# A transformer layer on one core: where the recurrent heads' element-wise work runs, on GpSimd, VectorE and ScalarE, and what it waits for

## The reference

```python
h = rms_norm(x, attn_norm_g)
qd, kd, vd, qr, fr, ir, gr = split(h @ w_in)             # 7 parts of 512 columns
od = rms_norm(diff_attention(norm(qd), norm(kd), vd, lam), subln_g) * (1 - lam_init)
lf = log_sigmoid(fr); kr = -expm1(lf); qr = silu(qr)     # recurrence: 4 heads, chunks
orr = hgrn2_chunked(qr, kr, ir, lf)                      # S_t = diag(f_t) S_(t-1) + k_t v_t^T
orr = rms_norm(orr, hgrn_norm_g) * silu(gr)
x = x + concat(od, orr) @ w_out
h = rms_norm(x, ffn_norm_g)
x = x + (silu(h @ w_gate) * (h @ w_up)) @ w_down
```

## Time and profile before

| what | value |
|---|---|
| median of the runs | 2820.31 us |
| the profiled execution's own time | 2819.41 us |
| its span | 2817.7 us |
| PE busy in the span | 2643.6 us (94%) |
| DVE, ACT, POOL busy | 1496.2, 1104.5, 758.5 us (53, 39, 27%) |
| granted PE clock, mean | 0.974 of full speed |

### The profile page before, as it was taken

One profiled execution on the slowest core, in us unless ns is written; L12 is line 12 of the kernel. 1 busy time (PEld: TensorE's weight loads), 2 busy tenths in 40 slices (PEclk: granted clock), 3 DMA queues, 4 the chain that ended last, 5 costly groups with the idle time before them and its releaser, 6 DMA issues. The chain is left out here.

```text
span 2817.7 us, 34114 instructions
## 1 busy us (share of the span) xinstructions
PE 2643.6 (94%) x13384; PEld 2235.7 (79%) x13384; DVE 1496.2 (53%) x1887; ACT 1104.5 (39%) x1871; POOL 758.5 (27%) x527
## 2 busy tenths in 40 slices
PE   7999999995999999987995999998999997999999
PEld 6888888885888888875884888887888886888887
DVE  5434343431676767663336655667566664456643
ACT  4434343331566666663234222224222222423221
POOL 5000000001424141400003544445544442146400
PEclk9999999997999999998997999999999998999999
DMA  4545455455443433206655333335333343787763
GB/s 162 196 164 179 136 183 176 148 179 157 107 105 105 105 106 83 76 8 207 194 198 202 112 103 100 104 102 196 109 100 104 101 112 91 254 293 253 253 213 126
DMA packets 338673, 415.78 MB, mean 148 GB/s; under 512 B 18513, under 2 KB 212049, under 8 KB 336721
## 3 DMA queue, kind: packets, MB, share of 16 engines
q1 hardware_dynamic: 338512, 413.60, 47.0%
HBM read 291.38 MB, written 122.16 MB: 147 GB/s over the span
## 5 line engine op out<-in xcount | busy, mean ns | idle before, releaser
L1846 PE MATMUL gate_bank<-gate_b_hi,gate_a_hi 128*128 128x512 f32 x1232 | 482.6, 392 | 37.1 <-DVE first_b_lo L1726 21.8
L1848 PE MATMUL gate_bank<-gate_b_hi,gate_a_lo 128*128 128x512 f32 x1232 | 481.4, 391 | 0.0
L1847 PE MATMUL gate_bank<-gate_b_lo,gate_a_hi 128*128 128x512 f32 x1056 | 412.4, 391 | 0.0
L1846 PEld LDWEIGHTS gate_bank<-gate_b_hi,gate_a_hi 128*128 128x128 f32 x1232 | 232.8, 189 | 87.5 <-issue 22.8
L1848 PEld LDWEIGHTS gate_bank<-gate_b_hi,gate_a_lo 128*128 128x128 f32 x1232 | 232.6, 189 | 48.6
L525 PE MATMUL proj_prod<-proj_w_hi,proj_h_hi 128*128 128x512 f32 x640 | 253.1, 395 | 6.8 <-DVE proj_w_lo L380 6.1
L2124 PE MATMUL down_prod<-down_w_hi,down_f_hi 128*128 128x512 f32 x616 | 241.4, 392 | 18.4 <-DVE down_f_lo L2060 18.2
L380 DVE TENSOR_TENSOR proj_w_lo<-proj_w_raw,proj_w_hi 128x2048 fp32r<-128x2048 f32 x56 | 128.7, 2299 | 230.1 <-ACT proj_w_hi L280 230.1
L527 PE MATMUL proj_prod<-proj_w_hi,proj_h_lo 128*128 128x512 f32 x640 | 250.1, 391 | 0.0
L526 PE MATMUL proj_prod<-proj_w_lo,proj_h_hi 128*128 128x512 f32 x640 | 249.8, 390 | 0.0
L2125 PE MATMUL down_prod<-down_w_lo,down_f_hi 128*128 128x512 f32 x616 | 240.7, 391 | 0.0
(11 more groups left out here) (212 smaller groups left out, 5548.8 us busy)
## 6 DMA issues: line engine op xcount, KB each, us to landing
proj_w_raw<-in_w_in_dram SPq DMA_DIRECT2D x56, 1024.0 KB, 6.4
first_full<-in_w_gate_dram SPq DMA_DIRECT2D x88, 256.0 KB, 3.9
gate_full<-in_w_up_dram SPq DMA_DIRECT2D x88, 256.0 KB, 4.0
ff<-gate_ff_sum SPq DMA_DIRECT2D x88, 256.0 KB, 2.9
down_w_raw<-in_w_down_dram SPq DMA_DIRECT2D x22, 1024.0 KB, 7.5
down_f_raw<-ff SPq DMA_DIRECT2D x56, 384.0 KB, 3.3
down_f_raw<-ff SPq DMA_DIRECT2D x56, 320.0 KB, 3.5
gate_b_lo<-operands SPq DMA_DIRECT2D x12, 1024.0 KB, 9.5
```

The lines of the kernel that those rows point to most:

```text
L1846: pe.matmul(dst, a_hi[:, pos, s, :], b_hi[pos][:, s, :], start=opens and s == 0, stop=False, skip_group_check=True)
L1847: pe.matmul(dst, a_hi[:, pos, s, :], b_lo[pos][:, s, :], start=False, stop=False, skip_group_check=True)
L1848: last = pe.matmul(dst, a_lo[:, pos, s, :], b_hi[pos][:, s, :], start=False, stop=s == HALF_SLABS - 1, skip_group_check=True)
```

## The change

Three things change in `mix_tokens`:

1. The recurrent chunks (4 to 7) are scaled by DVE instead of ACT: one TENSOR_TENSOR of 128x512 for each chunk, with `rec_o` and the inverse roots as inputs, in place of four ACT instructions of 128x128. It stands at the end of DVE's step, one step ahead of the transposition. In the last head ACT scales all four attention chunks before it copies the first chunk; before, it scaled one chunk ahead.
2. On POOL, `behind_combination` is gone, and so is the gate's wait for the combination.
3. On POOL, all seven factors of a head are made at the head's start, behind the gate of the head before.

```diff
--- before.py
+++ after.py
@@ -822,53 +822,29 @@
 
         @block.gpsimd
         def _(pool):
-            def product(h, m):
-                src = whole[m][:] if m else rf[:].rearrange("p h n -> p (h n)")
-                src = src.rearrange("p (n s) -> p n s", s=2)
-                if m:
-                    pool.wait_ge(whole_made, h * LEVELS + m)
-                nc.gpsimd.tensor_tensor(whole[m + 1][:], src[:, :, 0], src[:, :, 1], ALU.mult).then_inc(whole_made, 1)
-
-            def behind_combination(h, n):
-
-                step = h * STEPS + n // 2
-                if n % 2 == 0 and step:
-                    pool.wait_ge(combined, step)
-
-            def gate(h):
-                pool.wait_ge(rgate_in, 16 * (h + 1))
-                pool.wait_ge(fill_read, filled(h, len(FILLS) - 1))
-                if h + 1 < HEADS:
-                    pool.wait_ge(combined, (h + 1) * STEPS - 1)
-                nc.gpsimd.tensor_tensor(ro[:], ro[:], rgate[:], ALU.mult).then_inc(r_gated, 1)
-
             for h in range(HEADS):
-                if h == 0:
-                    pool.wait_ge(rf_in, 16)
-                    for m in range(LEVELS):
-                        product(h, m)
+                pool.wait_ge(rf_in, 16 * (h + 1))
+                for m in range(LEVELS):
+                    src = whole[m][:] if m else rf[:].rearrange("p h n -> p (h n)")
+                    src = src.rearrange("p (n s) -> p n s", s=2)
+                    if m:
+                        pool.wait_ge(whole_made, h * LEVELS + m)
+                    nc.gpsimd.tensor_tensor(whole[m + 1][:], src[:, :, 0], src[:, :, 1], ALU.mult).then_inc(whole_made, 1)
                 for side in range(2):
                     pool.wait_ge(fill_done, filled(h, fill_at("diagonal", side, HALF - 1)))
                     nc.gpsimd.tensor_tensor(half(rq, side), half(rq, side), half(rf, side), ALU.mult).then_inc(q_ready[side], 1)
                 for m in range(LEVELS):
                     for side in range(2):
-                        n = fill_at("level", side, m)
-                        pool.wait_ge(fill_done, filled(h, n))
-                        behind_combination(h, n)
+                        pool.wait_ge(fill_done, filled(h, fill_at("level", side, m)))
                         if m:
                             pool.wait_ge(k_ready[side], h * LEVELS + m)
                         nc.gpsimd.tensor_tensor(runs_of(rk, side, m, 0), runs_of(rk, side, m, 0), factor(side, m, 0), ALU.mult).then_inc(k_ready[side], 1)
                         pool.wait_ge(q_ready[side], h * UPDATES + m + 1)
                         nc.gpsimd.tensor_tensor(runs_of(rq, side, m, 1), runs_of(rq, side, m, 1), factor(side, m, 1), ALU.mult).then_inc(q_ready[side], 1)
-                if h + 1 < HEADS:
-                    pool.wait_ge(k_ready[1], (h + 1) * LEVELS)
-                    pool.wait_ge(q_ready[1], (h + 1) * UPDATES)
-                    pool.wait_ge(rf_in, 16 * (h + 2))
-                    for m in range(LEVELS - 1):
-                        product(h + 1, m)
-                    pool.wait_ge(fill_read, filled(h, len(FILLS) - 1))
-                    product(h + 1, LEVELS - 1)
-                gate(h)
+                pool.wait_ge(rgate_in, 16 * (h + 1))
+
+                pool.wait_ge(fill_read, filled(h, len(FILLS) - 1))
+                nc.gpsimd.tensor_tensor(ro[:], ro[:], rgate[:], ALU.mult).then_inc(r_gated, 1)
 
         @block.scalar
         def _(act):
@@ -927,19 +903,9 @@
                 nc.scalar.activation(o_rms[:], o_sumsq[:], ACT.Sqrt, bias=eps[:], scale=1.0 / P).then_inc(o_rms_made, 1)
 
             def normalise(h, c):
-
-                if c < TURNS:
-                    act.wait_ge(o_rrms_made, h + 1)
-                    for t in range(c * GROUP, (c + 1) * GROUP):
-                        nc.scalar.activation(o_all[h % 2][:, t, :], o_all[h % 2][:, t, :], ACT.Copy, scale=o_rrms[:, t:t + 1]).then_inc(o_normed, 1)
-                else:
-                    act.wait_ge(r_rrms_made, h + 1)
-                    act.wait_ge(r_gated, h + 1)
-                    head = c - TURNS
-                    for t in range(CH):
-                        part = ro[:, t, head * C:(head + 1) * C]
-                        at = t * HEADS + head
-                        nc.scalar.activation(part, part, ACT.Copy, scale=ro_rrms[:, at:at + 1]).then_inc(r_scaled, 1)
+                act.wait_ge(o_rrms_made, h + 1)
+                for t in range(c * GROUP, (c + 1) * GROUP):
+                    nc.scalar.activation(o_all[h % 2][:, t, :], o_all[h % 2][:, t, :], ACT.Copy, scale=o_rrms[:, t:t + 1]).then_inc(o_normed, 1)
 
             act.wait_ge(chain, 2)
             nc.scalar.activation(lam_exps[:], lam_dots[:], ACT.Exp).then_inc(lam_exp_made, 1)
@@ -966,13 +932,13 @@
                 if 0 < len(groups) <= 2:
                     read_output(s - 1)
                 if s == TOTAL + 1:
-                    normalise(HEADS - 1, 0)
+                    for c in range(TURNS):
+                        normalise(HEADS - 1, c)
                 for head, c in chunks_at(s):
-                    if s == TOTAL + 1 and c + 1 < CHUNKS:
-                        normalise(head, c + 1)
                     take_chunk(head, c)
                 for head, c in chunks_at(s + 1) if s < TOTAL else ():
-                    normalise(head, c)
+                    if c < TURNS:
+                        normalise(head, c)
 
         @block.vector
         def _(dve):
@@ -1035,6 +1001,16 @@
                 nc.vector.reciprocal(ro_rrms[:], ro_rms[:]).then_inc(r_rrms_made, 1)
                 dve.wait_ge(o_rms_made, h + 1)
                 nc.vector.reciprocal(o_rrms[:], o_rms[:]).then_inc(o_rrms_made, 1)
+
+            def normalise(h, c):
+
+                if c >= TURNS:
+                    dve.wait_ge(r_rrms_made, h + 1)
+                    dve.wait_ge(r_gated, h + 1)
+                    head = c - TURNS
+                    out = ro[:, :, head * C:(head + 1) * C]
+                    scale = ro_rrms[:].rearrange("p (c h) -> p c h", h=HEADS)[:, :, head]
+                    nc.vector.tensor_tensor(out, out, scale.unsqueeze(2).to_broadcast([P, CH, C]), ALU.mult).then_inc(r_scaled, 1)
 
             nc.vector.memset(state[:], 0.0)
             nc.vector.memset(early[:].bitcast(F32), 0.0).then_inc(masks_made, 1)
@@ -1068,6 +1044,8 @@
                     read_fill(h, 2 * j + 1)
                 if live and h and j == FIRST_CHUNK_STEP - 2 or s == TOTAL + 1:
                     invert_roots(h - 1)
+                for head, c in chunks_at(s + 1) if s <= TOTAL - 1 else chunks_at(s):
+                    normalise(head, c)
 
         @block.tensor
         def _(pe):
@@ -1118,7 +1096,7 @@
                 if c < TURNS:
                     pe.wait_ge(o_normed, h * STEPS + (c + 1) * GROUP)
                 else:
-                    pe.wait_ge(r_scaled, (h * HEADS + c - TURNS + 1) * CH)
+                    pe.wait_ge(r_scaled, h * HEADS + c - TURNS + 1)
                 open_slot(slot)
                 for t in range(GROUP):
                     src = o_all[h % 2][:, c * GROUP + t, :] if c < TURNS else ro[:, t, (c - TURNS) * C:(c - TURNS + 1) * C]
```

## The result

The change makes the kernel slower: 2838.47 us, median of 4 runs (2837.49 to 2840.85), against 2820.68 us, median of 4 runs before (2819.41 to 2823.25). The ratio is 1.0063 (1.0046 to 1.0081), +17.8 us. The forecast was 2844 us in a range of 2826 to 2854.

What follows compares the result with a forecast made beforehand. PE, busy 94% of the span, was taken as the bound, so new PE waits are time. 13.8 + 2.1 + 2.8 + 6.9 - 3.3 + 2.4 = 24.7 us slower than 2819.4 gave 2844 us, range 2826 to 2854.

Steps and rivals of the forecast that it cites:

- Step 5 of part 1: Heads 1 to 3: late DVE scalings let POOL's products hold L1000 and L1004; PE stalls 2.4 us, booked as 2.3 each.
- part 2: POOL's level products no longer wait for the combination: 2.1 us at step 7 plus 2.8 us at step 8.
- Step 6 of part 1: Heads 1 to 3, one step on: the same hold with a slightly shorter one on the second scaling, 2.3 us each.
- clock term: PE falls to its 1.2 GHz level after new waits: two more drops, 2.4 us, bounds 0 to 10.8.
- the clock falls after each new wait: Rival: 7 more clock drops of PE than taken, +8.4 us, 2852.5 us; chance 0.11.
- Step 7: All four heads: POOL's product or L1004 first, a draw; 0 or 1.05 us each, half taken, 2.1 us.
- Step 8: All four heads: POOL goes first, L1004 ends 1.05 us later, PE stalls 0.7 each; 2.8 us.
- Head ends: Three head ends: the next head's factor products hold L1000 and L1004, 2.3 us late each; 6.9 us.
- End of the stage: Last head: ACT scales 16 times, then copies, DVE scaling beside it; -3.3 us, bounds -5.5 and -1.7.
- The scalings slip through: Rival: both DVE scalings run ahead of POOL's q product, part 1's cost is zero; +9.3 us, 2829 us; chance 0.18.
- DVE is hardly held: Rival: DVE's queued pair L1000, L1004 keeps its turn against POOL; +1.8 us, 2821 us; chance 0.11.
- Faster, through ACT: Rival: ACT's lighter load shrinks PE's 26.2 us of waits for exponentials; 2801.5 us, or 2816 with the end alone; chance 0.05.

Runs made afterwards that it cites:

- scaling_alone: Kernel before, with only the recurrent chunks' scaling moved to DVE and the changed end of the stage; POOL as before: 2819.86 us, ratio 0.9995.
- wait_restored: Changed kernel, but POOL's side 0 level products wait for the combination again: 2823.80 us, ratio 1.0013 to the kernel before.
- one_input: Changed kernel, but in the first three heads DVE's scalings become sums over the same 128x512 elements with one SBUF input: 2825.80 us, ratio 1.0020 to before.
- act_scaling_in_heads: Changed kernel, but ACT does the recurrent scaling within the heads again; the end stays as changed: 2828.15 us, ratio 1.0030 to the kernel before.
- no_wait_alone: Kernel before, with only the wait of POOL's level products for the combination removed: 2827.96 us, ratio 1.0025.
- factors_alone: Kernel before, with only all seven factors made behind the gate and the gate's wait for the combination removed: 2826.20 us, ratio 1.0018.
- end_alone: Kernel before, with only the last head's eight chunks scaled as in the changed kernel: 2819.17 us, ratio 0.9993.
- end_all_dve: Kernel before, with DVE scaling all eight chunks of the last head, one instruction each, ACT only copying: 2814.61 us, ratio 0.9981.

## Why the prediction was right

The sign, the size and the order of the engines came out. Step by step:

**Step 5 of part 1** was right in mechanism and size: 2.2 us measured, 2.4 worked out and 2.3 booked. The chain is the one that the prediction wrote down: turns at step 4, k ahead of the small instruction, q ahead of the combination. But it hangs on both parts. By `scaling_alone` and `wait_restored` the late pair itself costs 0.59 us; the other 1.63 us are the holds on L966 (0.84) and L970 (0.79), which need part 1 to make DVE late and part 2 to let POOL go. The trace of after has POOL ahead by 0.05 us (865.51 against 865.56). The prediction booked the whole under part 1, and in the sum that made no difference. It had a margin that wasn't there: with DVE 1.1 us late its k product came 0.55 us ahead of L1000 (862.1 against 862.65), while in the trace DVE is 0.59 late and POOL 0.05 to 0.07 ahead. At step 6 a lead of 0.13 us for DVE was enough to turn the order, so the prediction was lucky that POOL still came first at step 5.

**Step 6 of part 1** was right in size by luck and wrong in cause. 2.3 each were forecast from a second hold. In the trace L966 and L970 keep their bare lengths there (0.22 and 1.02 us): behind the second pair DVE still waits for PE's scores (2.17, 1.20 and 1.84 us in heads 1 to 3), so the pair doesn't make it late, and the 3.3, 1.6 and 3.3 us come from PE at 1.2 GHz for 6.8, 3.4 and 6.8 us. The prediction's clock term (two drops, 2.4 us) was too small for steps 5 and 6, and the rival "the clock falls after each new wait" was right for the 2.1 us waits: it fell after three of three. It was wrong for the waits of 1.3 us and less: at steps 7 and 8 and at the head ends the kernel after has no drop. So two errors of about the same size offset each other: the hold of 6.9 that did not come, and a clock loss of 8.2 that did. For both steps and the clock together 16.2 us were forecast (13.8 + 2.4) and 14.8 measured (6.6 + 8.2). That the wait brings the drop about rests on its coming in three heads of three in the one profiled execution of the kernel after, and in none of the heads of `scaling_alone`, `wait_restored`, `one_input` and `act_scaling_in_heads`, where that wait is missing.

**Step 7** was called a draw and priced at half. POOL won it four times of four in the kernel after and again in `no_wait_alone`: 3.4 us for 2.1.

**Step 8**: 0.80 each, 3.2 us for 2.8.

**Steps 9 and 10** were not in the sum. They give back 5.5 us. Some 0.2 in each head is part of the hold of step 8 given back: `no_wait_alone` has the same 0.22, and so has head 3, behind which there are no factors to make. Part 3 gives next to nothing: the factor products no longer run beside the combination of step 9, whose L1004 took 1.86 us and in `factors_alone` takes 1.42, but `wait_restored`, which has part 3 without the hold, gains 0.05 us in head 2, where neither it nor before had a drop. The prediction took 0 for it. The rest is a clock drop that the profiled run of before had there in three of four heads, and the one of after had in none. The wait ahead of it is the same in both. First before, then after, head 0:

```profile
755.67 0.80 PE L1085 MATMUL att_ring<-att_k_first,att_q_hl 128*128 128x512 f32 x1 [2.29 <-ACT att_expo L879]
```

```profile
758.55 0.50 PE L1063 MATMUL att_ring<-att_k_first,att_q_hl 128*128 128x512 f32 x1 [2.29 <-ACT att_expo L855]
```

Behind the same 2.29 us the first matmul of 512 columns takes 0.80 or 0.50 us. Over the profiled runs these drops came in 0 to 4 of the four heads, at about 1.45 us each. What decides it is open.

**Head ends**: 1.87 each for 2.3, 5.6 us for 6.9. The hold was right (2.16 us late for 2.3). But the next step takes back 0.57, where the prediction let all of it through to the weighted sum, and 0.26 is lost again a step on; `factors_alone` has the same three numbers.

**End of the stage**: -4.0 us in the profile for -3.3, within the bounds. By the medians `end_alone` is worth 1.7, with an interval that reaches from -4.5 to +0.3. The prediction's own working here is a little off: 16 scalings to 1266.3, two copies at 0.7 and six at 1.1 us end at 1274.3 and not 1274.6, and eight copies at 0.7 give -5.9, not the -5.5 of its bound.

**The scaling instruction**: 0.61 us alone, 0.7 taken. **PE's wait for the combination**: 15.1 us more, where the prediction wrote some 21.

**The sum.** 24.7 us were forecast, 21.9 measured in the profiled execution, 17.8 by the medians. The parts alone (-1.0, +7.1 and +5.3) add up to 11.4; the 6.4 left are what the parts do to each other. The trace names more than that: 4.9 us of holds at step 5 (3 x 1.63) and some 7.7 of clock (8.2 less 3 x 0.15). Drops at step 9 that went (up to 4.4 in this pair of runs) bring it to 8.2; the remaining difference is inside the intervals of the ratios (about 2.5 us to either side for the parts, 5 for the kernel after).

The rivals fell by rows. "The scalings slip through": the pair takes 2.70 us with the q product inside. "DVE is hardly held": 15 waits of PE, 16.6 us. "Faster, through ACT": the wait for ACT is 26.2 us in both.

## What to carry to other kernels

Before an instruction with two SBUF inputs is moved to VectorE, look at what GpSimd does at that moment and at what stands behind it on VectorE: what counts is less its own length than who is late next, and whether the late one now meets GpSimd. Two edits that each look cheap can cost more together, so try them apart and together. A wait that makes the uncritical engine start after the critical instruction can be worth more than the work it delays: here it was 13.5 us.

## What the runs showed of the hardware

- The two engines took turns by whole instructions: two 128x512 instructions of DVE with two SBUF inputs, which met the last 0.58 us of one product and then a second one, took 2.70 us (alone 0.61 each), and the second product, bare 1.15, took 1.60. With one input the two took 1.27 us.
- An instruction on one number per partition pays the full price of a turn: 1.06 us for 0.22. GpSimd went first when both started within 0.01 us of each other (step 7, all heads of four kernels) and even at the head ends, where the recorded start of L970 is 0.03 us earlier than the second factor product's; VectorE went first when it was 0.13 us ahead (step 6).
- Three waits of PE of 2.1 us in an otherwise dense stretch were each followed by 3.4 or 6.8 us at 1.2 GHz (18 matmuls in 3.4 us, where the earlier trace rows has 26 in such a stretch); waits of 2.29 us elsewhere were or were not, from one execution to the next.
- Behind a wait of 14.0 to 15.0 us in every kernel, the first 7 us of the next stage ran at a granted clock of 0.57 to 0.60 (18 or 19 matmuls: `end_alone`, `one_input`, `act_scaling_in_heads`, `end_all_dve`) or of 0.73 to 0.80 (23 or 24 matmuls: the other six). How early the stage started doesn't sort them.
